# Three feed-forward layers with a convolution: products on x times the norm's weight, the norm's factor applied when PSUM is read, and the low halves of the down weights and of the gated activation moved to GpSimd

## What is computed

```python
def rmsnorm(x, g):
    xf = x.astype(jnp.float32)
    y = xf * lax.rsqrt(jnp.mean(xf * xf, axis=-1, keepdims=True) + RMS_EPS)
    return (y * g.astype(jnp.float32)).astype(x.dtype)
...
h = rmsnorm_3(x, norm_ffn)
u = causal_dwconv(h @ w_up, conv_w, conv_b)      # 1024 -> 2 * 2816, three taps over tokens
a, bval = jnp.split(u, 2, axis=-1)
return x + (jax.nn.silu(a) * bval) @ w_down      # 2816 -> 1024
```

## Time and profile before

| | |
|---|---|
| median of 3 runs | 2151.45 us (2143.9 to 2174.91) |
| profiled execution, first to last instruction (span) | 2150.0 us |
| granted TensorE clock over the span, mean | 0.988 |
| PE busy | 2122.7 us, 99% |
| DVE busy | 1437.0 us, 67% |
| ACT busy | 1158.6 us, 54% |
| POOL busy | 477.9 us, 22% |
| DMA | 438.95 MB, mean 204 GB/s |

### The profile page before, as it was taken

How to read it: one execution, slowest core, us unless ns; L and a number is a source line. 1 busy time by engine, 2 the same in 40 slices (tenths; PEclk the granted TensorE clock), 3 DMA queues, 4 the chain that set the end, 5 groups by cost and what they waited for, 6 DMA issues and landing times.

```text
span 2150.0 us, 47664 instructions
## 1 busy us (share of the span) xinstructions
PE 2122.7 (99%) x19346; PEld 2057.3 (96%) x19346; DVE 1437.0 (67%) x1972; ACT 1158.6 (54%) x1579; POOL 477.9 (22%) x254
## 2 busy tenths in 40 slices
PE   9999999999999999999999999999999999999998
PEld 8989999999999999988999999997999999999998
DVE  5666888657887899756899766567523454557554
ACT  6624655656666444664544544466544554556565
POOL 0030000100000355131354344310144400001443
PEclk9999999999999999998999999999999999999999
DMA  7223666444675787542788588644355453444552
GB/s 273 86 29 147 234 253 234 161 153 168 250 271 187 289 336 302 213 155 97 272 326 314 214 307 310 243 171 151 138 195 185 174 209 139 154 161 177 190 192 107
DMA packets 64391, 438.95 MB, mean 204 GB/s; under 512 B 7127, under 2 KB 9848, under 8 KB 12170
## 3 DMA queue, kind: packets, MB, share of 16 engines
q1 hardware_dynamic: 60480, 430.75, 54.0%
q10 hardware_dynamic: 3786, 6.38, 1.3%
HBM read 434.49 MB, written 2.62 MB: 203 GB/s over the span
## 4 chain that ended last, share of the span: by engine, by line
PE 91%; DVE 3%; ACT 3%; issue 1%; POOL 1%; DMA 0%; POOLq 0%; DVEq 0%
PE ps L346 25%; PE ps L348 25%; PE ps L347 25%; PE ps L360 1%; PE ps L368 1%; PE ps L362 1%; PE ps L1674 1%; PE ps L491 1%; PE ps L388 1%; ACT w_hi L284 1%; PE ps L390 1%; PE ps L389 1%; POOL hf L475 1%; PE ps L484 1%; PE ps L1696 1%
## 5 line engine op out<-in xcount | busy, mean ns | idle before, releaser
L346 PE MATMUL ps<-h_hi,w_hi 128*128 128x256 f32 x3412 | 956.3, 280 | 2.2 <-DVE h_lo L2442 1.3
L347 PE MATMUL ps<-h_lo,w_hi 128*128 128x256 f32 x3412 | 949.9, 278 | 0.0
L348 PE MATMUL ps<-h_hi,w_lo 128*128 128x256 f32 x3412 | 949.8, 278 | 0.0
L290 DVE TENSOR_TENSOR w_lo<-ring,w_hi 128x2048 fp32r<-128x2048 f32 x272 | 623.7, 2294 | 375.9 <-ACT w_hi L284 371.9
L284 ACT ACTIVATE w_hi<-ring 128x2048 fp32r<-128x2048 f32 x334 | 639.1, 1914 | 147.3 <-PE ps L348 142.7
L346 PEld LDWEIGHTS ps<-h_hi,w_hi 128*128 128x128 f32 x3412 | 644.6, 189 | 9.3 <-issue 6.5
L348 PEld LDWEIGHTS ps<-h_hi,w_lo 128*128 128x128 f32 x3412 | 644.9, 189 | 0.0
L347 PEld LDWEIGHTS ps<-h_lo,w_hi 128*128 128x128 f32 x3412 | 644.0, 189 | 0.2
L346 PE MATMUL ps<-g_hi,w_hi 128*128 (+1 forms) x1232 | 342.1, 278 | 1.6 <-POOL g_lo L894 0.9
L347 PE MATMUL ps<-g_lo,w_hi 128*128 (+1 forms) x1232 | 341.8, 277 | 0.0
L348 PE MATMUL ps<-g_hi,w_lo 128*128 (+1 forms) x1232 | 341.8, 277 | 0.0
(11 more groups left out here) (475 smaller groups left out, 2534.0 us busy)
## 6 DMA issues: line engine op xcount, KB each, us to landing
ring<-in_weights SPq DMA_DIRECT2D x334, 1024.0 KB, 4.8
mix<-in_modw SPq DMA_DIRECT2D x72, 1024.0 KB, 4.8
bias_rows<-below_mix ACTq DMA_DIRECT2D x1, 1536.0 KB
mix<-in_c_ssd ACTq DMA_DIRECT2D x1, 1536.0 KB, 8.1
x<-in_x SPq DMA_DIRECT2D x2, 512.0 KB, 3.8
ring<-in_weights SPq DMA_DIRECT2D x2, 512.0 KB, 6.5
...
```

Source lines behind the costliest of these rows:

```text
L290: dve.tensor_tensor(w_lo[:, n % SLOTS], ring[:, n % SLOTS], w_hi[:, n % SLOTS], ALU.subtract).then_inc(lo_ready[n % SLOTS], 1)
L346: pe.matmul(o, w[0], a_hi, start=first, stop=False, **kw)
L347: pe.matmul(o, w[0], a_lo, start=False, stop=False, **kw)
L348: return pe.matmul(o, w[1], a_hi, start=False, stop=last, **kw)
```

## The change

In ffn0, ffn1 and ffn6 (`scaled`) the products of the up units run on `x` times the norm's weight. ACT makes `h_hi` of each block straight from `x` behind each part of the residual (`scaled_act`), DVE makes `h_lo` (`scaled_dve`), and unit 0 starts on these. The sum of squares is formed meanwhile: POOL adds it down to two blocks (`scaled_pool`), PE sums those behind unit 0 (`scaled_pe_sums`) and spreads the factor over partitions in the middle of unit 1 (`norm_pe_over` as `mid`), and ACT copies it to `rstd`.

The factor comes in where the bank is read: `zs` is now made by DVE as bank times `rstd`, which gives the bank back, and ACT makes `acc` from `zs`, for which it waits for `z_free`. DVE makes `w_lo` of unit n+3 for every up unit right behind `zs`, ahead of the taps; the taps wait for `acc_done`. The product group of ffn0 and ffn1 now stands ahead of `gf`. `dve_alone` and `dve_glo` are empty, so POOL makes `g_lo` and the low half behind each down unit in all layers.

At the end of the program, while DVE makes the last norm, 30 products without effect on the output (`last_products`) take the place of two.

```diff
@@ three_blocks @@
-        dve_alone = ("ffn0", "ffn1")
+        dve_alone = ()
+        dve_glo = ()
+        scaled = ("ffn0", "ffn1", "ffn6")
@@ new functions @@
+        def scaled_act(act, tag, eps, gain, prev_last):
+            for q, (k, n) in enumerate(square_tiles(tag, KD)):
+                act.wait_ge(*after(f"dve:{STAGES[STAGES.index(tag) - 1]}.res{q}"))
+                for b in range(k, k + n) if tag != "ffn6" or q not in (1, 3) else () if q == 1 else (6, 2, 3):
+                    if tag == "ffn6" and b == 2:
+                        act.wait_ge(unit_done, prev_last + 1)
+                    act.activation(h_hi[:, b], x[:, b], ACT.Copy, scale=gain(b)).then_inc(*step(f"act:{tag}.hi{b}"))
+                act.activation(hf[:, k:k + n], x[:, k:k + n], ACT.Square).then_inc(*step(f"act:{tag}.sq{q}"))
+            act.activation(root[:, 2:3], eps_at[eps], ACT.Sqrt)
+        def scaled_pe_sums(pe, tag):
+            for k, w in ((0, "six"), (6, "pair3")):
+                pe.wait_ge(*after(f"pool:{tag}.{w}"))
+                done = token_sums(pe, ps[6], k, lambda c: slice(c, c + 1), ones[:, 0:1], int(k == 0), k == 6)
+            done.then_inc(*step(f"pe:{tag}.ss"))
...
@@ ffn_pe, up @@
-                a_unit(pe, n, m % 2, i, parts=parts if m == 0 else None)
+                a_unit(pe, n, m % 2, i, parts=parts if m == 0 else None,
+                       mid=(lambda: norm_pe_over(pe, name)) if m == 1 and name in scaled else None)
+                if m == 0 and name in scaled:
+                    scaled_pe_sums(pe, name)
@@ ffn_act, up @@
-                act.wait_ge(unit_done, n + 1 + i * 3)
+                if name in scaled:
+                    act.wait_ge(z_free, zbase[name] + m + 1 + i * 2)
+                    if 22 * c + m >= 2:
+                        act.wait_ge(g_done, 22 * f + m - 1 + i * 2)
+                else:
+                    act.wait_ge(unit_done, n + 1 + i * 3)
...
-                    act.activation(zs[:, e], ps[e][:].rearrange("p (a b) -> p a b", a=2), ACT.Copy)
+                    if name not in scaled:
+                        act.activation(zs[:, e], ps[e][:].rearrange("p (a b) -> p a b", a=2), ACT.Copy)
                     for half in range(2):
-                        done = act.activation(acc[:, e, half], ps[e][:, half * T:(half + 1) * T], ACT.Identity,
+                        src = zs[:, e, half] if name in scaled else ps[e][:, half * T:(half + 1) * T]
+                        done = act.activation(acc[:, e, half], src, ACT.Identity,
...
-                    done.then_inc(z_free, 1)
+                    if name in scaled:
+                        done.then_inc(acc_done, 1)
+                    else:
+                        done.then_inc(z_free, 1)
@@ ffn_dve, up @@
-                    dve.wait_ge(z_free, zbase[name] + m + 1 + i * 2)
+                    if name in scaled:
+                        if m == 0:
+                            dve.wait_ge(*after(f"act:{name}.over"))
+                        dve.wait_ge(unit_done, n + 1 + i * 3)
+                        dve.tensor_tensor(zs[:, e], ps[e][:].rearrange("p (a b) -> p a b", a=2), by_block(rstd[:], 2),
+                                          ALU.mult).then_inc(z_free, 1)
+                        if m < KF - 1:
+                            lo(dve, n + SLOTS, i)
+                        dve.wait_ge(acc_done, 22 * scaled.index(name) + m + 1 + i * 2)
+                    else:
+                        dve.wait_ge(z_free, zbase[name] + m + 1 + i * 2)
...
-                if m % 2 == 0:
+                if m % 2 == 0 and name not in scaled:
                     lo(dve, n + SLOTS, i)
+                if name in scaled:
+                    products(m, i)
                 dve.wait_ge(silu_done, 22 * f + m + 1 + i * 2)
```

More of the change, by code:

```diff
@@ L355, in a_unit @@
             if parts:
-                for k in range(ks):
+                for k in scaled_order(parts, ks):
                     pe.wait_ge(*after(f"act:{parts}.hi{k}"))
@@ L427, in norm_act, with scaled_order, scaled_pool, scaled_dve @@
                 norm_act_parts(act, tag, kb, shift, dst)
+        def scaled_order(tag, ks):
+            return (0, 1, 4, 5, 6, 2, 3, 7) if tag in scaled and tag == "ffn6" else range(ks)
+        def scaled_act(act, tag, eps, gain, prev_last):
[7 more added lines that the diff above has]
+            act.activation(root[:, 2:3], eps_at[eps], ACT.Sqrt)
+        def scaled_pool(pool, tag):
+            for name, a, b, waits in (("pair0", 0, 1, ("act:{}.sq0",)), ("pair1", 2, 3, ("act:{}.sq1",)),
+                                      ("quad", 0, 2, ("pool:{}.pair0", "pool:{}.pair1")), ("pair2", 4, 5, ("act:{}.sq2",)),
+                                      ("six", 0, 4, ("pool:{}.quad", "pool:{}.pair2")), ("pair3", 6, 7, ("act:{}.sq3", "act:{}.sq4"))):
+                for w in waits:
+                    pool.wait_ge(*after(w.format(tag)))
+                pool.tensor_tensor(hf[:, a], hf[:, a], hf[:, b], ALU.add).then_inc(*step(f"pool:{tag}.{name}"))
+        def scaled_pe_sums(pe, tag):
[3 more added lines that the diff above has]
+            done.then_inc(*step(f"pe:{tag}.ss"))
+        def scaled_dve(dve, tag, gain):
+            for q in range(4):
+                for b in (2 * q, 2 * q + 1):
+                    dve.wait_ge(*after(f"act:{tag}.hi{b}"))
+                    done = dve.scalar_tensor_tensor(out=h_lo[:, b], in0=x[:, b], scalar=gain(b), in1=h_hi[:, b],
+                                                    op0=ALU.mult, op1=ALU.subtract)
+                done.then_inc(*step(f"dve:{tag}.lo{q}"))
         def square_tiles(tag, kb):
@@ L512, in norm_pe, with last_products @@
             norm_pe_over(pe, tag)
-            keep_warm(pe, 2, warm, tag)
+            if tag.startswith("fin"):
+                last_products(pe)
+            else:
+                keep_warm(pe, 2, warm, tag)
+        def last_products(pe):
+            for j in range(8):
+                pe.matmul(ps[1 + j % 2][:, 0:T], w_hi[:, 0, P * j:P * j + P], h_hi[:, j], start=True, stop=True)
+            for j in range(8):
+                pe.matmul(ps[1][:, 0:P], w_hi[:, 0, P * j:P * j + P], h_hi[:, j, 0:P], start=True, stop=True)
+            for j in range(8):
+                pe.matmul(ps[1][0:64, 0:T], w_hi[:, 0, P * j:P * j + 64], h_hi[:, j], start=True, stop=True)
+            for j in range(6):
+                pe.matmul(ps[1][:, 0:384], w_hi[:, 0, P * j:P * j + P], g_hi[:, 2 * j:2 * j + 2].rearrange("p k t -> p (k t)")[:, 0:384],
+                          start=True, stop=True)
         def norm_pe_twice(pe, tag, sums, warm):
@@ L862, in up @@
                 dve.tensor_tensor(gf[:, e], val, sil[:, e], ALU.mult).then_inc(g_done, 1)
-                if m % 2 == 1 and m < KF - 1:
+                if m % 2 == 1 and m < KF - 1 and name not in scaled:
                     lo(dve, n + SLOTS, i)
-                if name in dve_alone:
+                if name in dve_glo:
                     dve.wait_ge(ghi_done, 22 * f + m + 1 + i * 2)
@@ L896, in down @@
             def down(j, n, i):
-                if j < 9:
+                if j < 9 and name not in dve_alone:
                     lo(pool, n + SLOTS, i)
@@ L2890, in _ @@
                 for i, s in enumerate(STAGES):
+                    if s in scaled:
+                        scaled_act(act, s, 1e-6, norm_of[s][0], last_unit[STAGES[i - 1]])
+                        hi(act, owed)
+                        norm_act_root(act, s, D, 1e-6)
+                        act.wait_ge(*after(f"pe:{s}.over"))
+                        act.activation(rstd[:], ps[7][:, 0:T], ACT.Copy).then_inc(*step(f"act:{s}.over"))
+                        owed = last_unit[s] + SLOTS
+                        ffn_act(act, s)
+                        continue
                     norm_act(act, s, x, KD, D, 1e-6, source_ready(i), shift=norm_of[s][1],
@@ L2942, in _ @@
                         owed = last_unit[s] + 2
-                    if s.startswith("ffn") and s not in dve_alone:
+                    if s.startswith("ffn") and (s not in dve_alone or s not in dve_glo):
                         ffn_pool(pool, s)
```

28 lines of the change are left out of this document (25 added, 3 removed).

## The result

The changed kernel takes 2336.19 us (median of 6 runs, 2321.96 to 2346.85), the kernel before beside it 2154.39 us (6 runs). The ratio is 1.082, with a 95% interval of 1.076 to 1.088. The forecast was 2322 us. The profiled execution took 2326.13 us, its span is 2324.3 us, 174.3 more than before.

A forecast was written before the change was run, and what follows sets the result against it. PE bounds the kernel before; afterwards a serial round of DVE and ACT does. Span 2150.0 + 170.2 (layers) - 0.6 (starts) + 1.2 (handoffs) = 2320.8 us, plus 1.45 around it: 2322 us, 7.9% slower, range 2300 to 2345.

The forecast's parts named there:

- What bounds the layer: In ffn0, ffn1 and ffn6 PE bounds before; after the change DVE and ACT work serially, and no busy sum sets pace.
- The round: One up unit's zs, acc, w_hi, w_lo, taps, sil and gf run one after another: 8.44 us against PE's 5.44.
- the term for handoffs in the loop: Waits cost about 0.1 us more; two new handoffs in eight odd rounds of three layers: +4.8 us, net +1.2.
- The down unit: Behind odd units m = 3 to 19, ACT's w_hi for the unit behind a down unit delays acc: +1.69 us.
- POOL's exclusion: Behind a down unit, DVE's w_lo waits out POOL's low half: 1.77 us more, 47.8 us over 27 rounds.
- The product group: In ffn0 and ffn1, now between taps and gf, it adds 2.33 us in each of nine rounds a layer.
- A shared bandwidth: If DVE and POOL shared SBUF bandwidth instead of locking: about half the wait, some 22 us less over three layers.
- The layers: From first zs to last gf: ffn0 +59.6, ffn1 +65.8, ffn6 +44.8 us, together +170.2.
- The start of a layer: The first zs still waits for the factor: 0.6 us off for three layers together, bounds +3 to -6.
- Rival 3: TensorE's clock falls as PE idles; half of each turn at 1.2 GHz adds 77 us, 2400 us; chance 0.06.

## Why the prediction was right, step by step

**What bounds the layer.** Right: no engine's sum of busy time, but a ring of handoffs that DVE and ACT take in turns. That the length is the order's and not the work's is shown by the two runs that keep the scaled products and come back to turns of 17 us: one leaves out most of POOL's low half, the other leaves out nothing and gives DVE more work (in its ffn1 DVE still sets the pace, at 17.0).

**The round.** Its six steps measure 0.34, 0.87, 1.00, 1.93, 2.21 and 2.32 us, against 0.34, 0.72, 0.90, 1.94, 2.21 and 2.33 predicted. Two were short by 0.15 and 0.10, and the term for handoffs in the loop, 0.2 for each odd round, made up for them: 8.64 with it, 8.67 measured (8.74 in ffn6). That is in part luck: `acc` itself takes 1.09 us when it reads `zs`, where it took 1.01 from the bank, and this is no handoff.

**The down unit.** `acc` starts 2.68 us after `gf` (predicted 2.75), DVE's `w_lo` 5.59 (predicted 5.59), POOL ends at 7.38 (predicted 7.5). `w_lo` was predicted to be busy 4.06 and is busy 3.93 to 3.99. The round measures 11.85 us in ffn6 (2208.22 to 2220.07), predicted 11.90.

**POOL's exclusion.** Predicted 1.77 us a turn, and 1.7 is what cutting POOL's instruction short gives back. The Trainium skill, page "SBUF — State Buffer", section on who interferes with whom, adds that the order of issue decides who blocks, not the size of the operation. The trace agrees: the small addition blocked for 4.16 us, and POOL's own instruction took 5.44 us, not 4.5, where it was issued at 697.31 into a reduction of DVE's that ran from 696.59 to 698.34.

**The product group.** Predicted 4.66 us from the first tap to `gf`, measured 4.50 (342.79 to 347.29). A turn of ffn0 was predicted at 22.7, measured 22.64.

**A shared bandwidth.** The prediction says that it would about halve POOL's term, some 22 us less. No row gives this, and half of 47.8 us is 24. The forecast didn't use it, and in each meeting with a POOL low half shown here DVE was done only when POOL's instruction was over.

**The layers.** +59.6, +65.8 and +44.8 predicted, +58.75, +64.88 and +45.62 measured: 170.2, or 171.4 with the handoffs, against 169.3. The errors lie on both sides: ffn0 and ffn1 were taken 0.9 us too long, ffn6 0.8 too short.

**The start of a layer.** Predicted to bring 0.6 us in three layers, as the first `zs` is the start of the chain and still needs the factor. It waits 2.9 us for `rstd` in each of them, and in ffn0 it moved by 0.07. This is the term that had the wrong sign. From the last `gf` of ffn0 to the first `zs` of ffn1 it is 133.2 us in both profiles of the kernel before and 132.5 with `scaled` empty, but 134.9 to 136.9 in all eight traces with scaled products. So about 2 us of loss there belong to the change; which of its steps costs them no run shows.

**What was missed.** The stretches outside the three layers are 5.1 us longer than before (0 to the first `zs`, the two between layers, and the end, from 16.2 to 17.8 us), where I had 0.6 less. The 2 us between ffn0 and ffn1 belong to the change (above). The rest can't be put down to it: the stretch between ffn1 and ffn6 took anything from 1274.9 to 1303.0 us over the traces, mostly by the spacing of the matmuls, and the end is 16.2 to 16.5 us long in five of the other versions with scaled products and 17.8 and 18.8 in two. The remaining 10 us lie between the profiled execution (2326.13) and the median (2336.19), which I had taken to be as close as in the kernel before.

**Rival 3.** Its mechanism came, its price didn't. The clock is 0.83 to 0.92 in many of the turns and the matmuls of the down units average 302 ns, where they averaged 278. So PE stands still for 3.6 to 3.9 us in the turns of ffn0 and ffn1 shown, not for the 6 predicted. But at full clock PE has 4 to 6 us to spare in each turn, and turns at 0.83 and 1.00 have the same length. In ffn6 it is close: at 2208.81 `zs` was held up by PE's unit for 0.16 us.
